# One core, two model blocks and a routed expert layer: sums of squares, scores, weighed values and the router's choice reordered

## The chip, the core and the metric

The kernel runs on one core of a Trainium2 chip. The metric is the device time of one execution in microseconds. Engines: PE is TensorE (PEld its weight loads), DVE is VectorE, ACT is ScalarE, POOL is GpSimd, SP is SyncE, which issues the DMAs. All of them run their own instruction streams and meet only at semaphores.

## What is computed

256 tokens of width 1024, float32, pass through two blocks. The first has a state-space branch (a complex linear scan over 64 groups of 64 states), a dilated attention of three groups of eight heads, and two gates. The second has another recurrent branch, a difference attention and a layer of 32 experts in 4 groups of 8, of which each token uses two of one group.

```
h = rms_norm(x, norm_w);  u, z_s, q, k, v, z_a, r_s, r_a = split(h @ w_in)
y = scan(u) @ C + d_skip * u;  g = gelu(y);  y_s = (g * sigmoid(g @ w_glu) * silu(z_s)) @ w_ssm_out
q, k = rope(rms_norm(q)), rope(rms_norm(k));  y_a = (attention(q, k, v) * silu(z_a)) @ w_attn_out
x = x + (sigmoid(r_s) * y_s + sigmoid(r_a) * y_a) @ w_o
... second block of the same kind, then
g_sel = argmax(xn @ w_rg + b_rg)                    # of 4 groups
e_in_group = (xn @ w_re + b_re)[g_sel]              # 8 logits
top_v, top_i = top_k(e_in_group, 2)
x = x + sum over the two of weight * (silu(xn @ w1[e]) * (xn @ w3[e])) @ w2[e]
```

## The kernel before, in words

All engines' programs are written by hand, each in one order; helper objects give the waits. `Banks` (L112) numbers the uses ("fills") of two PSUM banks: `to_fill` makes PE wait until the fill before on the same bank was read, `filled` and `emptied` signal, `to_read` and `after_read` wait. `pj` has banks 0 and 1, `tp` 2 and 3, `tq` bank 2.

**Start** (L542 to L635, L763 to L788, L949 to L1005). SP issues the first constants, the turned x (1 MB, one semaphore), the first half of u's weights (1 MB, `u_half`), the second half, the state-space matrices and u's second unit. ScalarE issues four small loads (gains of q and k, positions), squares x in four pieces of 512 columns (L619), takes the root of the row sums (L622). DVE multiplies x by the norm gains (L962, `raw`), takes the reciprocal (L966, `rows1`), scales `raw` to `hT` in eight steps (L969) and u's block 0 (L971); then it works through the phases, the rotary angles and the decay factors (L981 to L1005) up to `prm_ready`. PE warms up on constants (L765), sums the squares over the partitions with a matrix of ones (L768, eight products), then makes u in eight blocks (L784): block 0 from `raw`, the rest from `hT`. A float32 product shows as two instructions. ScalarE takes blocks 1 to 7 of u out of PSUM (L629).

**Scan stage** (43 to 240 us). The state-space part goes by 16 pairs. `inputs_of_two_pairs` (L794) and `outputs_of_two_pairs` (L805) run on PE. For each pair ScalarE makes sines and cosines (`trig`, L636 to L642), DVE rotates and scans (L1045 to L1061), POOL turns the states back (L594 to L599) and signals `state_ready`. `trig(n)` waits for `state_ready` of pair n - 2, as its tables are shared by two pairs. Before its first pair, POOL scales the output matrices with the decay factors (L582 to L586): it starts at `prm_ready` and ends with `c_scaled`. Between these, PE makes 26 half units of q, k, v and the gates r (`DENSE`, L323 and L332) in 18 steps h (`HALVES`). ScalarE copies each out (L691), takes the squares of q and k (L695) and their roots (L700); DVE norms and rotates them (`norm_rope`, L1076 to L1084); PE turns them (L856, from h = 5 on, one of 12 in each step), and ScalarE copies them to `qT`, `kT` (L706). The last step, h = 17, makes the last two half units and, between them, the last outputs and `scores(0)`.

**Attention** (248 to 301 us). Eight steps: `scores(a + 1)` (L818), a quarter of z_s (L339), `weigh_values(a - 1)` (L881), `turn_p(a)` (L869). DVE masks, finds the maximum and norms (L1120 to L1131), ScalarE takes exponentials (L667) and copies the turned probabilities (L721), DVE copies the outputs (`take_output`, L1138). Then `weigh_values(7)`, and the eight products of glu (L339).

**Router and experts** (647 us to the end). DVE adds the bias to the logits (L1599) and chooses: `first_largest` (L1602 to L1607) marks the first of the largest values by four linked steps, once for the group and twice for the experts. L1622 writes `aexp`, the 0/1 table of the chosen experts; PE counts places by triangular and full matrices of ones (L1445 to L1449), DVE makes the selection (L1631), PE gathers the tokens (L1512) and multiplies (L1532, L1559, L1564, L1578). The expert weights, 192 MB in units of 2 MB, come through a ring of eight slots; SP's loads L371 and L373 wait until PE has used the units before (`unit_used`). Loads up to the eleventh unit are issued before the router ends.

## Time and profile before

| | |
|---|---|
| median of 3 runs | 1091.53 us (1090.1 to 1091.58) |
| the profiled execution, own time | 1091.93 us |
| its span, first to last instruction | 1090.1 us |
| PE busy | 951.0 us (87%) |
| DVE, ACT, POOL busy | 407.5, 257.3, 157.3 us |
| mean granted clock of PE | 0.939 |
| DMA moved | 292.93 MB, mean 269 GB/s |

The page cuts the span in 40 slices of 27 us; a digit is the busy share in tenths. PE is at 9 until the 25th slice (about 680 us), the DMA row is at 9 from the 23rd to the last but one:

```profile
PE   8999999999999999999999998966665867676756
DMA  9444244242234447643224789999999999999997
```

### The profile page before, as it was taken

Reading aid. Unit: us, or ns where it says so; the run is one execution under the profiler, and the core shown is the slowest. Engines: PE = TensorE matmul, PEld = TensorE weight load, DVE = VectorE, ACT = ScalarE, POOL = GpSimd, SP = SyncE. Lnnn points to the kernel's source line nnn. Section 1 sums busy time; section 2 is a strip of 40 time slices with the busy share of each in tenths; the row PEclk is TensorE's granted clock in tenths of the full one; section 3 lists DMA queues with packets and bytes.
Section 4 is the critical chain, followed back from the end, with each engine's and each line's share of the span. In section 5 each row is a group of like instructions: output and inputs, shape, how many; then the busy total and the mean of one; then the engine's idle time right before and its main releaser. Section 6 shows DMA issues by size and latency. Waiting matters only on the chain.

```text
span 1090.1 us, 12714 instructions
## 1 busy us (share of the span) xinstructions
PE 951.0 (87%) x5108; PEld 560.0 (51%) x5108; DVE 407.5 (37%) x701; ACT 257.3 (24%) x629; POOL 157.3 (14%) x107
## 2 busy tenths in 40 slices
PE   8999999999999999999999998966665867676756
PEld 7655645568888857545788753423221313131312
DVE  6779899836621113263633222210110102020201
ACT  3595977423411021312312020000000000000000
POOL 0976777830000000000000000000000000000000
PEclk9999999999999999999999999988887878897988
DMA  9444244242234447643224789999999999999997
GB/s 356 194 154 154 79 155 155 99 176 85 91 141 155 155 155 256 232 153 125 88 98 155 322 339 378 430 427 423 427 427 425 430 427 429 429 426 429 427 429 313
DMA packets 29777, 292.93 MB, mean 269 GB/s; under 512 B 8480, under 2 KB 9376, under 8 KB 10912
## 3 DMA queue, kind: packets, MB, share of 16 engines
q1 hardware_dynamic: 28640, 292.21, 66.1%
q8 instruction: 33, 0.54, 0.2%
q10 hardware_dynamic: 1088, 0.05, 0.1%
q14 instruction: 16, 0.13, 0.0%
HBM read 291.20 MB, written 1.05 MB: 268 GB/s over the span
## 4 chain that ended last, share of the span: by engine, by line
PE 60%; DMA 32%; ACT 3%; DVE 2%; issue 2%; POOL 1%; SPq 0%; DVEq 0%; ACTq 0%; POOLq 0%
DMA mem<-in_experts 32%; PE psum L332 15%; PE psum L339 8%; PE psum L323 8%; PE psum L311 6%; PE psum L316 5%; PE psum L1532 3%; PE psum L784 3%; PE psum L1858 1%; PE psum L1559 1%; PE psum L818 1%; PE psum L881 1%; PE psum L1549 1%; PE psum L869 1%; PE psum L1512 1%
## 5 line engine op out<-in xcount | busy, mean ns | idle before, releaser
L1532 PE MATMUL psum<-mem 128*32 128x512 f32 x1012 | 151.9, 731 | 79.7 <-DMA mem<-in_experts 79.6
L323 PE MATMUL psum<-mem,hT 128*128 128x512 f32 x288 | 126.3, 595 | 0.8 <-ACT mem L629 0.8
L1532 PEld LDWEIGHTS psum<-mem 128*32 128x32 f32 x1012 | 31.6, 122 | 181.6 <-DMA mem<-in_experts 112.0
L332 PE MATMUL psum<-hT,mem 128*128 128x256 f32 x512 | 115.2, 381 | 0.0
L332 PEld LDWEIGHTS psum<-hT,mem 128*128 128x128 f32 x512 | 95.6, 190 | 15.9 <-issue 2.9
L323 PEld LDWEIGHTS psum<-mem,hT 128*128 128x128 f32 x288 | 55.7, 196 | 64.8 <-issue 64.8
L332 PE MATMUL psum<-mem 128*128 128x256 f32 x320 | 69.7, 379 | 0.0
L311 PE MATMUL psum<-mem,hT 128*128 128x512 f32 x160 | 69.2, 592 | 0.0
L1677 DVE SCALAR_TENSOR_TENSOR mem<-mem,psum 128x512 f32<-128x512 f32 x8 | 5.5, 686 | 158.6 <-ACT mem L1429 158.6
L332 PEld LDWEIGHTS psum<-mem 128*128 128x128 f32 x320 | 60.6, 190 | 8.1
L1559 PE MATMUL psum<-mem 128*32 128x512 f32 x256 | 41.2, 777 | 22.9 <-DMA mem<-in_experts 18.7
L339 PE MATMUL psum<-hT,mem 128*128 128x256 f32 x256 | 57.6, 382 | 0.0
L316 PE MATMUL psum<-mem 128*128 128x512 f32 x128 | 55.6, 592 | 0.0
L1427 ACT ACTIVATE mem<-psum 128x256 f32<-128x256 f32 x8 | 3.1, 384 | 214.6 <-PE psum L1540 214.6
L339 PEld LDWEIGHTS psum<-hT,mem 128*128 128x128 f32 x256 | 48.0, 190 | 7.0
L311 PEld LDWEIGHTS psum<-mem,hT 128*128 128x128 f32 x160 | 30.2, 190 | 36.9 <-issue 36.8
L1061 DVE TENSOR_TENSOR_SCAN mem<-mem 128x512 f32<-128x512 f32 x32 | 49.0, 1569 | 0.0
L1686 DVE TENSOR_TENSOR xres<-xres,psum 128x256 f32<-128x256 f32 (+1 forms) x48 | 24.5, 510 | 54.6 <-PE psum L1549 54.3
L1549 PE MATMUL psum<-mem 128*128 128x256 f32 (+1 forms) x96 | 36.6, 505 | 7.2 <-DVE mem L1682 7.2
L316 PEld LDWEIGHTS psum<-mem 128*128 128x128 f32 x128 | 24.2, 190 | 28.8 <-issue 28.7
L1512 PE MATMUL psum<-mem,xn 128*128 128x128 f32 x256 | 32.7, 289 | 6.6 <-issue 6.4
L1512 PEld LDWEIGHTS psum<-mem,xn 128*128 128x128 f32 x256 | 32.1, 205 | 8.3 <-issue 7.9
(362 smaller groups left out, 1197.3 us busy)
## 6 DMA issues: line engine op xcount, KB each, us to landing
mem<-in_experts SPq DMA_DIRECT2D x86, 2048.0 KB, 35.5
mem<-in_front SPq DMA_DIRECT2D x39, 2048.0 KB, 7.8
mem<-in_experts SPq DMA_DIRECT2D x18, 1024.0 KB, 33.0
mem<-in_front SPq DMA_DIRECT2D x2, 1024.0 KB, 10.3
xn<-in_xT SPq DMA_DIRECT2D x1, 1024.0 KB, 7.1
mem<-in_ssm_b SPq DMA_DIRECT2D x2, 512.0 KB, 12.5
mem<-in_ssm_c SPq DMA_DIRECT2D x2, 512.0 KB, 17.9
xres<-in_x SPq DMA_DIRECT2D x1, 1024.0 KB, 10.0
```

What stands on the lines that cost most here:

```text
L311: ins = pe.matmul(dst, lhs[:, k, P * i:P * i + P], w[:, k, c0:c0 + 512], start=(k == 0), stop=(k == nk - 1))
L316: ins = pe.matmul(dst, lhs[:, k, P * i:P * i + P], w[:, k, c0:c0 + 512], start=(k == 0), stop=(k == lhs.shape[1] - 1))
L323: ins = pe.matmul(dst, tokens[:, k, i], w[:, k, :], start=(k == 0), stop=(k == KD - 1))
L332: ins = pe.matmul(dst[:, at:at + T], w[:, k, P * m:P * m + P], rhs[:, k, :], start=(k == 0), stop=(k == nk - 1))
L339: ins = pe.matmul(dst, w[:, k, P * m:P * m + P], rhs[:, k, :], start=(k == 0), stop=(k == nk - 1))
L784: ins = pe.matmul(pj.tile(s)[:, 0:256], w[:, m, k, :], (hT if s else raw)[:, k, :], start=(k == 0), stop=(k == KD - 1))
L1061: ins = dve.tensor_tensor_scan(out=dst[:, b], data0=decay_[:, 512 * b:512 * b + 512], data1=src, initial=0.0, op0=ALU.mult, op1=ALU.add)
L1512: ins = pe.matmul(bank[:, P * (k % 4):P * (k % 4) + P], xn[:, i, P * k:P * k + P], sel_[:, P * i:P * i + P], start=(i == 0), stop=(i == 1))
L1532: ins = pe.matmul(banks[m // 2 % 2][32 * q:32 * q + 32, :], xgT[:, k, 32 * q:32 * q + 32], w[q][:, FF * kk:FF * kk + FF], start=(k == 0), ...
L1549: pe.matmul(total(n), selT_[:, P * i:P * i + P], y_[:, at:at + width], start=True, stop=True).then_inc(combined, 1)
L1559: ins = pe.matmul(banks[2][r, :], hidT[:, k, r], w[q][:, 512 * kk:512 * kk + 512], start=(k == 0), stop=(k == 3), tile_position=(0, 32 * q))
L1686: dve.tensor_tensor(dst, dst, total(n), ALU.add).then_inc(added, 1)
```

## The change

1. The sum of squares: x arrives by two halves (`xT_in[0]`, `xT_in[1]`), u's first blocks by two loads of 512 KB (`u_block_in`). DVE adds the four pieces of squares to one (three additions of 512 columns, `sq_added`), and PE needs two products with ones for it, behind u's block 0. Block 1 too is made from `raw` and scaled by DVE (`scale_u`). Warm-up products: five, not six. The gains of q and k come with the constants, so three of ScalarE's four small loads are gone; the first constants are 56 KB shorter.
2. PE's waits on the last two blocks of u and on `c_scaled` ahead of step h = 0 move to h = 2 and to the first outputs; ScalarE's on `c_scaled` to its first copy into `qT`.
3. In step 17 the last outputs stand ahead of the last half unit, and `scores(0)` between its two blocks.
4. `weigh_values(7)` stands behind the first product of glu.
5. The router ranks: for each logit the number of larger ones, and equal ones of lower index, is summed; rank 0 is the first choice, rank below 2 the two chosen. The table of places takes two products with 64 columns where three had 32. What the weights need (maxima, differences) comes behind the selection, and the weights' chain behind the first gathered tokens.

```diff
         def sync_of_first_layer(sp):
...
-            sp.dma_start(x_turned, A["xT"]).then_inc(xT_in, 16)
-            sp.dma_start(ring[:, 0, 0:2048], A["front"][0, :, 0:2048]).then_inc(u_half, 16)
+            for n in range(2):
+                sp.dma_start(x_turned[:, 4 * n:4 * n + 4, :], A["xT"][:, 4 * n:4 * n + 4, :]).then_inc(xT_in[n], 16)
+            for n in range(2):
+                sp.dma_start(ring[:, 0, 1024 * n:1024 * n + 1024], A["front"][0, :, 1024 * n:1024 * n + 1024]).then_inc(u_block_in[n], 16)
...
         def scalar_of_first_layer(act):
-            for c, name in enumerate(("q_norm_w", "k_norm_w")):
-                act.dma_start(qkw[:, 3 * c:3 * c + 3, :], A[name][0, :, 0:16].partition_broadcast(P)).then_inc(misc_in, 16)
-            act.dma_start(qk_col, A["qk_columns"]).then_inc(misc_in, 16)
             act.dma_start(posi[:, :], A["att_positions"]).then_inc(misc_in, 16)
...
-            for j in range(1, 4):
+            for j in range(2, 4):
                 take_u(j)
...
-            act.wait_ge(c_scaled, 1)
-            act.wait_ge(misc_in, 64)
+            act.wait_ge(con2_in, 16)
...
                         tq.to_read(act, s)
+                        if s == 0:
+                            act.wait_ge(c_scaled, 1)
...
-            for n in range(6):
+            for n in range(5):
                 pe.matmul(banks[7][:, 0:256], ident, con[:, 0:256], start=True, stop=True)
-            for k in range(KD):
-                pe.wait_ge(sq_done, k // 2 + 1)
-                ins = pe.matmul(tp.tile(TP_X)[:, 0:256], C("ones"), squares[:, 256 * k:256 * k + 256], start=(k == 0), stop=(k == KD - 1))
-            tp.filled(ins, TP_X)
+            def sum_of_squares():
+                pe.wait_ge(sq_added, 3)
+                for k in range(2):
+                    ins = pe.matmul(tp.tile(TP_X)[:, 0:256], C("ones"), squares[:, 256 * k:256 * k + 256], start=(k == 0), stop=(k == 1))
+                tp.filled(ins, TP_X)
...
-            for m in range(4):
+            project_u(0, 0)
+            sum_of_squares()
+            for m in range(1, 4):
                 project_u(0, m)
...
-            for s in range(2):
-                pj.after_read(pe, PJ_U + 6 + s)
-            pe.wait_ge(c_scaled, 1)
             for h in range(STEPS):
+                if h == 2:
+                    for s in range(2):
+                        pj.after_read(pe, PJ_U + 6 + s)
...
                 for d in dense_of(h):
-                    if h == STEPS - 1 and d == dense_of(h)[1]:
-                        outputs_of_two_pairs(PAIRS // 2 - 1)
-                        for s in range(2):
-                            tq.after_read(pe, 10 + s)
-                        scores(0)
                     w = unit_ready(pe, DENSE[d // 2])
                     s = PJ_QKV + d
                     pj.to_fill(pe, s)
-                    if DENSE[d // 2][0] in "qkv":
+                    if h == STEPS - 1 and d == dense_of(h)[1]:
+                        outputs_of_two_pairs(PAIRS // 2 - 1)
+                        project_turned(pe, w, (2 * (d % 2),), pj.tile(s), hT)
+                        for q in range(2):
+                            tq.after_read(pe, 10 + q)
+                        scores(0)
+                        ins = project_turned(pe, w, (2 * (d % 2) + 1,), pj.tile(s), hT)
+                    elif DENSE[d // 2][0] in "qkv":
...
+            pe.wait_ge(g_ready, 2)
+            glu_gate(0)
             weigh_values(ATT_STEPS - 1)
-
-            pe.wait_ge(g_ready, 2)
-            for m in range(8):
...
+            for m in range(1, 8):
+                glu_gate(m)
...
+                for n in range(2):
+                    dve.wait_ge(sq_done, 2 * n + 2)
+                    a, b = (squares[:, 512 * m:512 * m + 512] for m in (2 * n, 2 * n + 1))
+                    dve.tensor_tensor(a, a, b, ALU.add).then_inc(sq_added, 1)
+                dve.wait_ge(sq_added, 2)
+                dve.tensor_tensor(squares[:, 0:512], squares[:, 0:512], squares[:, 1024:1536], ALU.add).then_inc(sq_added, 1)
...
+                scale_u(0)
                 for k in range(KD):
                     dve.tensor_tensor(hT[:, k, :], raw[:, k, :], rows1, ALU.mult).then_inc(hT_ready, 1)
-                pj.to_read(dve, PJ_U)
-                pj.emptied(dve.tensor_tensor(uT[:, 0, :], pj.tile(PJ_U)[:, 0:256], rows1, ALU.mult), PJ_U)
+                scale_u(1)
...
+            def ranks(out, x, n, lower, beats):
+
+                larger, equal = beats[:, :, :, 0], beats[:, :, :, 1]
+                other, own = bc(x.unsqueeze(2), [P, 2, n, n]), bc(x.unsqueeze(3), [P, 2, n, n])
+                mark(dve.tensor_tensor(equal, other, own, ALU.is_equal), dve3)
+                link(dve, dve.tensor_tensor(larger, other, own, ALU.is_gt), dve3)
+                first = bc(lower.rearrange("p (e f) -> p e f", e=n).unsqueeze(1), [P, 2, n, n])
+                step(dve.tensor_tensor(equal, equal, first, ALU.mult))
+                step(dve.tensor_reduce(out, beats.rearrange("p i e v f -> p i e (v f)"), AX.X, ALU.add))
...
-            step(dve.tensor_reduce(m1, eg, AX.X, ALU.max))
-            first_largest(oh1, eg, m1, C("rev8"), 8, t8)
-            step(dve.scalar_tensor_tensor(out=eg2, in0=oh1, scalar=NEG, in1=eg, op0=ALU.mult, op1=ALU.add))
-            step(dve.tensor_reduce(m2nd, eg2, AX.X, ALU.max))
-            first_largest(oh2, eg2, m2nd, C("rev8"), 8, t8)
-            step(dve.tensor_tensor(s8, oh1, oh2, ALU.add))
-            dve.tensor_tensor(by_group(aexp), bc(s8.unsqueeze(2), [P, 2, 4, 8]), of_group, ALU.mult).then_inc(chosen, 1)
...
+            ranks(rank, eg, 8, C("lower8"), beaten)
+            for i in range(2):
+                dve.scalar_tensor_tensor(out=by_group(aexp)[:, i], in0=bc(rank[:, i].unsqueeze(1), [P, 4, 8]), scalar=2.0,
+                                         in1=of_group[:, i], op0=ALU.is_lt, op1=ALU.mult).then_inc(chosen, 1)
```

## Rows read from the trace of the kernel before

**Rows 1.** Stretches: us, busy us (instructions) of PE, PEld, DVE, ACT, POOL, granted clock, DMA share, GB/s.

```profile
100.00:200.00 100.00, 99.56 (x450) 59.31 (x452) 91.76 (x105) 75.14 (x205) 77.40 (x53) 1.00 0.36 129
800.00:1000.00 200.00, 134.38 (x888) 43.99 (x888) 22.48 (x40) 7.59 (x17) 0.00 (x0) 0.80 1.01 428
```

**Rows 2.** PE's waits: line, released by, us in total, times, longest.

```profile
PE psum L1445 <- DVE mem L1622: 1.2, 1, 1.2
PE psum L323 <- ACT mem L629: 0.8, 1, 0.8
PE psum L881 <- ACT mem L721: 0.8, 1, 0.8
PE psum L818 <- ACT mem L691: 0.8, 1, 0.8
PE psum L856 <- ACT mem L706: 0.4, 1, 0.4
```

**Rows 3.** Time order, the start: start, duration, engine, line, operation, count [idle before].

```profile
4.42 5.49 PE L765 MATMUL psum<-con 128*128 128x256 f32 x12 [4.42 <-DMA con<-in_constants]
9.70 4.08 PE L768 MATMUL psum<-mem,con 128*128 128x256 f32 x16
...
13.61 3.62 PE L784 MATMUL psum<-xres,mem 128*128 128x256 f32 x16
...
14.32 1.75 DVE L966 RECIPROCAL mem<-mem 128x256 f32<-128x256 f32 x1 [3.76 <-ACT mem L622]
...
18.80 0.42 DVE L971 TENSOR_TENSOR mem<-psum,mem 128x256 f32<-128x256 f32 x1
```

**Rows 4.** Issue to landing of L544 (x, from 1.2) and L545 (u, from 1.7).

```profile
DMA to landing us min/median/max: 7.1/7.1/7.1
DMA to landing us min/median/max: 9.2/9.2/9.2
```

**Rows 5.** Time order, the chain beside PE, 28 to 113 us.

```profile
28.17 2.23 POOL L582 TENSOR_TENSOR mem<-mem 128x1024 f32<-128x1024 f32 x1 [27.72 <-DVE mem L1005]
...
51.60 1.60 POOL L599 TENSOR_TENSOR mem<-mem 128x512 f32<-128x512 f32 x1
...
53.31 0.62 ACT L636 ACTIVATE mem<-small 128x510 f32<-128x510 f32 x1
...
91.83 1.72 POOL L594 TENSOR_TENSOR mem<-mem 128x512 f32<-128x512 f32 x1 [7.56 <-issue]
...
102.85 0.63 ACT L636 ACTIVATE mem<-small 128x510 f32<-128x510 f32 x1 [4.69 <-POOL mem L599]
...
112.37 0.63 PE L856 MATMUL psum<-con,xres 128*128 128x128 f32 x4 [0.44 <-ACT mem L706]
```

**Rows 6.** Time order of PE in the expert stage.

```profile
758.84 3.24 PE L1532 MATMUL psum<-mem 128*32 128x512 f32 x16 [2.98 <-DMA mem<-in_experts]
```

**Rows 7.** Stretches of half a microsecond around it, columns as in rows 1.

```profile
758.00:758.50 0.50, 0.00 (x0) 0.00 (x0) 0.00 (x0) 0.00 (x0) 0.00 (x0) 0.64 1.08 459
761.00:761.50 0.50, 0.50 (x8) 0.00 (x0) 0.00 (x0) 0.00 (x0) 0.00 (x0) 0.50 0.92 393
```

**Rows 8.** Time order around the first scores.

```profile
238.72 1.15 PE L818 MATMUL psum<-mem 64*128 64x256 f32 x12
...
242.71 0.72 ACT L667 ACTIVATE mem<-mem,small 128x512 f32<-128x512 f32 x1 [8.68 <-DVE small L1124]
...
247.01 0.60 ACT L691 ACTIVATE mem<-psum 128x512 f32<-128x512 f32 x1 [2.30 <-PE psum L332]
```

**Rows 9.** DVE's copy of the last weighed values.

```profile
301.56 0.30 DVE L1138 COPY mem<-psum 128x128 f32<-128x128 f32 x1 [2.66 <-PE psum L881]
```

**Rows 10.** Time order of DVE in the router.

```profile
652.88 0.27 DVE L1615 TENSOR_REDUCE mem<-mem 128x16 f32<-128x64 f32 x1
...
655.67 0.23 DVE L1622 TENSOR_TENSOR mem<-mem 128x64 f32<-128x64 f32 x1
```

**Rows 11.** The microsecond of the expert stage's first ring load, columns as in rows 1.

```profile
663.00:664.00 1.00, 1.00 (x16) 0.28 (x11) 0.00 (x0) 0.00 (x0) 0.00 (x0) 1.00 0.00 0
```

More of the change, by code:

```diff
@@ L81, in constants @@
     put("ones", 1.0)
-    put("rev4", 4.0 - np.arange(4)[None, :])
-    put("rev8", 8.0 - np.arange(8)[None, :])
+    for n in (4, 8):
+        put(f"lower{n}", np.tri(n, n, -1).reshape(1, n * n))
     return c
@@ L440, in build @@
         ropcos = small[:, 582:598].rearrange("p (i n) -> p i n", i=2)
-        hss = [small[:, 972 + 16 * n:988 + 16 * n] for n in range(3)]
+        hss = [small[:, 148 + 16 * n:164 + 16 * n] for n in range(3)]
         hrs = [small[:, 646 + 16 * n:662 + 16 * n] for n in range(3)]
@@ L781, in project_u @@
                         pe.wait_ge(raw_ready, k + 1)
[L782 removed]
+                    elif s == 2:
                         pe.wait_ge(hT_ready, k + 1)
[L784 removed]
+                    ins = pe.matmul(pj.tile(s)[:, 0:256], w[:, m, k, :], (raw if s < 2 else hT)[:, k, :], start=(k == 0), stop=(k == KD - 1))
                 pj.filled(ins, s)
@@ L801, in outputs_of_two_pairs @@
                     pe.wait_ge(y_free.sem, j)
+                else:
+                    pe.wait_ge(c_scaled, 1)
                 for n, (CT, H) in enumerate(((CTr, Hr), (CTi, Hi))):
@@ L1649, in vector_of_experts @@
             step(dve.tensor_tensor(p1, p1, gw, ALU.mult))
-            for n in range(2):
-                dve.wait_ge(gather_full, n + 1)
-                take(2 * n, 2, banks[2 + 2 * n], xg_low)
             step(dve.tensor_tensor(p2, p1, ediff, ALU.mult))
```

96 lines of the change are left out of this document (55 added, 41 removed).

## The prediction

> **What bounds the kernel now.** I read the table of stretches first. From about 665 us on the DMA engines are busy all the time (share 1.01) while TensorE (PE) is busy two thirds of it; between 100 and 200 us it is PE that is full, 99.56 of 100 us [rows 1]. So the span is a PE stage of some 650 us followed by a stage that only streams expert weights. A microsecond saved in front of the stream moves the end by a microsecond if it lets PE issue or release something earlier, or the stream start earlier. The list of PE's waits shows what is to be had in front: 0.8 us at the first q projection (L323), 0.4 us at the turning of q and k (L856), 0.8 us at the scores (L818) and 0.8 us at the weighed values (L881) [rows 2]. After that I read the time order around each edited place, and, because a wait of PE that is removed is worth only what the next one leaves, the chain of work between 28 and 112 us.
>
> **Start: sum of squares on DVE, u's first block ahead of it.** Before, 12 warm-up matmuls (6 products, two passes each) run from 4.42 to 9.70, 0.44 us apart, 16 sum-of-squares instructions run until 13.61, and then 64 instructions of u follow, 16 in 3.46 us [rows 3]. After, there are 10 warm-ups (until 8.8), 16 of u's block 0, 4 of the sum. Block 0 needs the first 512 KB of u; its first 1024 KB landed 9.2 us after an issue at 1.7, at 10.9, and the 1024 KB of x ahead of them 7.1 after 1.2, at 8.3 [rows 4]: 2.6 us for 1024 KB. 512 KB less is 1.3 us; the shorter constants and the missing small loads of ScalarE's queue may give 0.2 to 0.7 more. So I take 9.0 for its start (8.8 to 9.9). The 16 instructions from 9.70 to 13.61 fit 0.43 us each until 10.6 and 0.216 after: there PE's clock rose from 1.2 to 2.4 GHz, after it had worked without a stop from 4.42. The 20 instructions then end at 10.6 + (20 - 3.7) x 0.216 = 14.1 instead of 13.6, and block 2 starts at 17.6 instead of 13.61 + 2 x 3.46 = 20.5. **PE is 2.9 us ahead** (2.3 to 3.1). The three additions of 512 columns (0.69 us each, two of them 0.6 apart) end at 11.7 on a DVE that was idle then: they cost nothing, and would cost from 13 us on. The removal of the waits on the last reads of u and on `c_scaled` at 43.5 adds what PE waited there, the 0.8 us of [rows 2]; the first product that comes after needs only u's last block but one to be read, which ScalarE did 2 us earlier. PE would be some 3.5 us ahead (3.1 if a part of that wait stays).
>
> **But the chain beside PE gets later.** The row factor comes 0.5 us later (14.1 against 13.6), its reciprocal is 1.75 us as before, and two blocks of u (0.42 us, 0.35 apart) are now scaled by DVE where one was [rows 3]. What follows on DVE without a pause ends in `prm_ready`, so that is 0.5 + 0.35 = **0.85 us later** (0.6 to 1.6). GpSimd (POOL) sat idle for 27.7 us until exactly that, at 28.17, and then works without a pause to the end of its first pair at 51.60 + 1.60 = 53.20; ScalarE's `trig(2)` starts at 53.31, because it needs that pair [rows 5]. From there ScalarE, then DVE (through 91.7), then POOL's fifth pair from 91.83, ScalarE's `trig(6)` from 102.85 (4.69 us idle for POOL) and its copy L706 follow each other, and at 112.37 PE waits 0.44 us for that copy [rows 5]. None of them waits for PE on the way after 53.3. An earlier PE doesn't make them earlier: it arrives between 108.4 and 108.8 and waits. A later POOL makes them later; some of the 0.85 is given back, as POOL's third pair starts on a DVE that is not late, so I take **+0.6 us** at 112 (0 to +1.5). The whole lead is thus lost there, and PE's stop is 0.4 + 3.3 + 0.6 = 4.3 us long (a little of it may fall earlier, at a bank that ScalarE copies late).
>
> **What the stop costs beyond itself.** In the last stage PE stood still for 2.98 us, until 758.84 [rows 6], and the granted clock went from 1.00 to 0.50 (1.2 GHz) within the half microsecond from 758.0 and was still there between 761.0 and 761.5 [rows 7]. At 1.2 GHz a matmul takes double (0.43 against 0.216 us, above). The stop of 1.2 us at L1445 [rows 2] left the clock at 1.00. A stop of 4.3 us lies above both, so I expect the clock to fall in it and about 3 us of work to be done at half pace: **+1.5 us** (0 to 3). The Trainium skill (TensorE: Matmul & The Clock Gate, What's actually happening) says that the throttled state is the default and that activity releases it, which speaks against a change that moves PE's waits into one long one; by it the cost would be as above, without it 0. The rows agree with it.
>
> **First scores inside the last projection.** Before: last outputs, scores(0) at 238.72, then 32 instructions of projection. After, 16 of those (3.46 us) go ahead of the scores. Neither PE nor anybody else waited at 238.72. But ScalarE stands behind it: it does nothing for 8.68 us until the maximum of these scores is there, takes the exponentials at 242.71, and only then copies the last two projections; the second copy started at 247.01, when PE delivered [rows 8]. Now the exponentials start at 246.17, the two copies at 247.60 and 248.10, and end at 248.70 instead of 247.61. PE waits for the second (`after_read` ahead of scores(1)), so its 0.8 us of [rows 2] become 1.9: **+1.1 us** (0.9 to 1.2). DVE's part has 5 us of slack ahead of the first turned probabilities, so nothing else follows.
>
> **Last weighed values behind a gate product.** PE waited 0.85 us for ScalarE's copy at 300.43; now 16 instructions of glu (3.46 us) cover that, and the bank they write is that of the weighed values before, emptied by then. But the second glu product needs the bank of these weighed values, which DVE empties by a 0.30 us copy right after them [rows 9]. Before, glu 0 stood between; now nothing does: 0.04 + 0.30 + 0.13 = 0.47 us of wait. **-0.4 us** (-0.85 to 0).
>
> **Router by ranks.** From the end of the reduction L1615 at 653.15 to the end of L1622 at 655.90 DVE makes 13 steps in 2.75 us [rows 10]. After: compare, compare, multiply on 128 elements each (between the 0.23 us of 64 and the 0.42 of 256: 0.30), a reduction of 256 to 16 elements (64 took 0.27; no row has 256 so: 0.45 to 0.6), two writes of 32 elements (0.19). With 0.035 us between linked steps and an overlap of 0.08 between unlinked ones: 0.22 + 0.33 + 0.33 + 0.5 + 0.3 = 1.7. The group rank costs as much as the first largest (1.0 against 1.06). PE's table of places needs 4 instructions instead of 6 (-0.2). `sel_ready` comes 1.0 - 0.06 + 0.2 = **1.15 us earlier** (0.5 to 1.5). This counts although the stream bounds: the load that waits for the second expert unit was issued at 663.13, and in 663 to 664 us the DMA engines moved nothing [rows 11]; the hole was 1.8 us. It shrinks by the gain, and all later issues go with PE.
>
> **Sum.** +0.6 + 1.5 + 1.1 - 0.4 - 1.15 = +1.65 us. The profiled execution took 1091.93 us, 1.8 around a span of 1090.1, and would take 1093.6; it lies 0.4 above the median of 1091.53, so I predict a median of **1093.2 us**.
>
> **Rivals.** *The clock holds through the stop*: all else as above, +0.15, 1091.7. For it: no row shows a stop of just this length. *PE keeps its lead*: if the chain at 112 is not binding, -3.5 + 1.1 - 0.4 - 1.15 = -3.95, 1087.6. For it: PE's stage is 99.5% full [rows 1] and the wait at 112 was only 0.4 us, so a slightly quicker POOL frees part. Against it: `trig(2)` can't start before POOL's first pair, whatever PE does. *The clock rises late at the start* (slower than before): between the warm-ups and u's block 0 PE stands still for 0.2 to 1 us before its clock has risen. If the rise comes 3.4 us later for that (as long as the low stretch of [rows 7], 758.1 to 761.5), the 20 instructions end 1.7 us later, at 15.8, DVE and POOL with them, and 112 us is reached at +2.3: in all +3.35, 1094.9. It decides as soon as block 0 lands after the last warm-up. *The stream hides the router*: if its start goes by landing times and not by the issue at 663.13, the 1.15 us fall away: +2.8, 1094.3. Against it: the hole of [rows 11].
>
> **Chances.** Forecast 0.38, clock holds 0.18, lead kept 0.17, late rise 0.14, router hidden 0.13. About 0.2% (2.2 us) is what a measurement of this kernel can tell from no change. Faster by more: the lead kept and a little of the second, 0.19. Slower by more, above 1093.7: a third of the forecast's own spread (1091.9 to 1094.7), most of the last two: 0.34. Within: 0.47. The range takes the upper half of the lead-kept case and the late rise with one microsecond of spread: 1088.5 to 1096.0.
>
> **What would show it.** At the start: block 0 of u from about 9 us, the sum's 4 instructions ending near 14, block 2 at 17.6. POOL's first instruction at 29.0. No wait of PE at 40, but one of 4 us for L706's successor near 109 to 113, with a granted clock of 0.5 behind it. ScalarE's last two copies adjoining near 248.6 and a PE wait of 1.9 us ahead of scores(1). 0.5 us ahead of the second glu product. The select of the first group 1.1 us nearer to the logits, and a DMA hole of 0.7 us. The prediction is wrong above all if `trig(2)` starts before 53 us of the old time scale, or if PE's long wait is absent.

## The result: slower by half a per cent, and the profile after

The changed kernel takes 1097.77 us (median of five runs; the kernel before 1091.29 beside it), ratio 1.0055, 95% interval 1.0043 to 1.0067. One of the five runs took 1186.88 us at a lower mean clock and is not in the ratio. The prediction said 1093.2, with a range of 1088.5 to 1096.0. The profiled span grew from 1090.1 to 1095.9 us.

**The start.** Time order of the kernel after (start us, duration us, engine, line, operation, count, idle before and what ended it); it answers to [rows 3] and to the first of [rows 5]:

```profile
3.29 4.64 PE L774 MATMUL psum<-con 128*128 128x256 f32 x10 [3.29 <-DMA con<-in_constants]
9.72 6.67 PE L795 MATMUL psum<-xres,mem 128*128 128x256 f32 x16 [1.80 <-DMA mem<-in_front]
16.23 1.03 PE L779 MATMUL psum<-mem,con 128*128 128x256 f32 x4
17.09 3.62 PE L795 MATMUL psum<-xres,mem 128*128 128x256 f32 x16
20.55 7.09 PE L795 MATMUL psum<-hT,mem 128*128 128x256 f32 x32
...
17.80 1.75 DVE L993 RECIPROCAL mem<-mem 128x256 f32<-128x256 f32 x1 [6.60 <-ACT mem L630]
...
31.98 2.22 POOL L593 TENSOR_TENSOR mem<-mem 128x1024 f32<-128x1024 f32 x1 [31.53 <-DVE mem L1037]
```

The warm-ups start 1.1 us earlier than before and end at 7.93; u's block 0 has landed only at 9.72. Behind the hole of 1.80 us the block takes 6.67 us, where the next one, with as many instructions, takes 3.62: nearly all of it ran at half pace. So the sum of squares ends at 17.2, the reciprocal starts at 17.80 instead of 14.32, and POOL at 31.98 instead of 28.17: **3.8 us late**. 3.5 of them are there at the reciprocal; the scaling of a second block adds 0.3 (13.85 us from reciprocal to POOL before, 14.18 after). Block 2 starts at 20.55; worked out for the kernel before it was 20.5. PE's lead is nil.

**The turn near 112 us.** First four rows of the kernel before that none of the groups above has, in the same form:

```profile
119.71 7.07 PE L332 MATMUL psum<-hT,mem 128*128 128x256 f32 x32
247.75 1.15 PE L818 MATMUL psum<-mem 64*128 64x256 f32 x12 [0.78 <-ACT mem L691]
656.91 0.42 DVE L1631 TENSOR_TENSOR mem<-con,psum 128x256 f32<-128x256 f32 x1 [0.87 <-PE psum L1447]
659.43 0.62 PE L1532 MATMUL psum<-hT,mem 128*32 128x512 f32 x2
```

and the kernel after, time order at the same places:

```profile
57.44 0.63 ACT L644 ACTIVATE mem<-small 128x510 f32<-128x510 f32 x1 [5.11 <-POOL mem L610]
...
72.68 7.14 PE L338 MATMUL psum<-hT,mem 128*128 128x256 f32 x32 [1.21 <-ACT xres L698]
...
116.10 1.09 PE L873 MATMUL psum<-con,xres 128*128 128x128 f32 x4 [3.78 <-ACT mem L715]
116.98 9.30 PE L329 MATMUL psum<-mem,hT 128*128 128x512 f32 x16
126.12 4.05 PE L338 MATMUL psum<-hT,mem 128*128 128x256 f32 x18
...
255.40 1.15 PE L831 MATMUL psum<-mem 64*128 64x256 f32 x12 [1.82 <-ACT mem L698]
...
312.19 3.05 PE L345 MATMUL psum<-mem 128*128 128x256 f32 x13 [0.49 <-DVE mem L1170]
...
666.46 0.62 PE L1568 MATMUL psum<-hT,mem 128*32 128x512 f32 x2 [1.00 <-DMA hT<-in_experts]
```

`trig(2)` starts at 57.44 (53.31 in [rows 5]), the turn at 116.10 (112.37): the 3.8 us of POOL arrive there whole, as +3.73. PE stands still for 3.78 us ahead of it. Its wait of 0.85 us at 43.52, which the second edit was to remove, is gone, but a wait of 1.21 us at 72.68 has come for it: PE reaches the turn at 112.32, and had reached it at 111.93 before. The granted clock of the stretches behind (us from and to, length, busy and count of PE, clock, DMA share, GB/s):

```profile
113.00:115.00 2.00, 0.00 (x0) 0.93 0.00 0
115.00:117.00 2.00, 0.90 (x5) 0.50 0.00 0
```

It fell to 0.50 (1.2 GHz) in the stop, and the next projection starts at 126.12 instead of 119.71, +6.41: the clock costs another 2.7 us in this execution. At the second scores it is 255.40 against 247.75, +7.65, so the moved scores cost 1.2 more. The wait of the second glu product is 0.49 where PE had waited 0.85 for the weighed values.

**The router.** DVE's selection starts 4.29 us after the second logits (658.59 to 662.88) instead of 5.57 (651.34 to 656.91): 1.28 us gained. But the first product on expert weights waits 1.00 us for the landing of its weights and comes at 666.46 against 659.43, +7.03. Nearly all the gain is gone within 4 us: the logits were 7.25 us late, so 0.2 is left of it. At the end of the span +5.8 is left; the other 1.2 us lie in the streaming stage. In the ninth run below a kernel that starts its first expert unit at the same 659.42 as the kernel before ends 0.9 us earlier, so single executions differ by that much there; what makes the 1.2 us is open.

### The profile page after: what moved, and what is told of

It reads as the page before. It is cut to its first block, busy times and chain, and to the rows that moved or that the text cites. A ratio compares the mean times of both kernels' runs of the same rounds, so it can differ in the third digit from the quotient of the medians.

```text
span 1095.9 us, 12684 instructions
## 1 busy us (share of the span) xinstructions
PE 948.0 (87%) x5092; PEld 558.9 (51%) x5092; DVE 406.9 (37%) x705; ACT 257.1 (23%) x628; POOL 157.6 (14%) x107
## 4 chain that ended last, share of the span: by engine, by line
PE 56%; DMA 33%; POOL 3%; DVE 3%; ACT 2%; issue 2%; SPq 0%; DVEq 0%; POOLq 0%; ACTq 0%
DMA mem<-in_experts 32%; PE psum L338 15%; PE psum L345 8%; PE psum L329 7%; PE psum L317 6%; PE psum L322 5%; PE psum L1568 3%; PE psum L1901 1%; PE psum L1595 1%; PE psum L831 1%; PE psum L898 1%; PE psum L1585 1%; PE psum L886 1%; DMA hT<-in_experts 1%; DMA mem<-in_front 1%
## 5 line engine op out<-in xcount | busy, mean ns | idle before, releaser
L1568 PE MATMUL psum<-mem 128*32 128x512 f32 x1012 | 146.3, 707 | 84.4 <-DMA mem<-in_experts 84.4
L329 PE MATMUL psum<-mem,hT 128*128 128x512 f32 x288 | 128.5, 603 | 0.0
L317 PE MATMUL psum<-mem,hT 128*128 128x512 f32 x160 | 69.2, 592 | 0.0
L1595 PE MATMUL psum<-mem 128*32 128x512 f32 x256 | 43.7, 819 | 20.7 <-DMA mem<-in_experts 17.2
```

Source lines behind the costliest of these rows:

```text
L317: ins = pe.matmul(dst, lhs[:, k, P * i:P * i + P], w[:, k, c0:c0 + 512], start=(k == 0), stop=(k == nk - 1))
L329: ins = pe.matmul(dst, tokens[:, k, i], w[:, k, :], start=(k == 0), stop=(k == KD - 1))
L1568: ins = pe.matmul(banks[m // 2 % 2][32 * q:32 * q + 32, :], xgT[:, k, 32 * q:32 * q + 32], w[q][:, FF * kk:FF * kk + FF], start=(k == 0), ...
L1595: ins = pe.matmul(banks[2][r, :], hidT[:, k, r], w[q][:, 512 * kk:512 * kk + 512], start=(k == 0), stop=(k == 3), tile_position=(0, 32 * q))
```

## The experiments

Each was timed in at least five runs beside the kernel before; all ratios are to the kernel before unless said otherwise. Rows and waits are those of one profiled execution of each kernel, so they tell how that execution went; the ratios tell what the kernels cost. Where two are compared, each carries an interval of about 0.001.

### First run: the start of the kernel before

```diff
-            for n in range(5):
+            for n in range(6):
                 pe.matmul(banks[7][:, 0:256], ident, con[:, 0:256], start=True, stop=True)
+            for k in range(KD):
+                pe.wait_ge(sq_done, k // 2 + 1)
+                ins = pe.matmul(tp.tile(TP_X)[:, 0:256], C("ones"), squares[:, 256 * k:256 * k + 256], ...)
+            tp.filled(ins, TP_X)
...
-            project_u(0, 0)
-            sum_of_squares()
-            for m in range(1, 4):
+            for m in range(4):
                 project_u(0, m)
```

(with the one load of x, the first 1024 KB of u in one load, and block 1 from `hT`.)

> The changed kernel with the start of the kernel before (x and u's first 1024 KB by one load each, six warm-up products, eight products of squares ahead of u's block 0, ScalarE takes block 1); the moved waits, the scores, the weighed values and the router stay changed. Theory (the loss comes from the start: the sum of squares ends 3.5 us late, so POOL, ScalarE and PE's turn near 112 us are late, and the stop lets the clock fall): POOL's first instruction near 28.2, PE's stop at the turn 1.0 to 1.3 us at 112.4 with the clock at 1.00 behind it, and against the kernel before +1.2 (scores) -0.4 (weighed values) -0.2 to -1.15 (router): 1091.0 to 1091.9 us, ratio 0.9997 to 1.0006. Rival A (the moved scores and the removed waits make the loss): about 1097, ratio 1.005. Rival B (the router pays in full and the scores cost nothing): 1089.8, ratio 0.9986.

Measured: ratio 0.9981 (0.9972 to 0.9990), 1089.67 us. Time order:

```profile
11.61 3.62 PE L790 MATMUL psum<-xres,mem 128*128 128x256 f32 x16
...
26.18 2.23 POOL L589 TENSOR_TENSOR mem<-mem 128x1024 f32<-128x1024 f32 x1 [25.73 <-DVE mem L1022]
...
109.94 0.63 PE L866 MATMUL psum<-con,xres 128*128 128x128 f32 x4 [1.11 <-ACT mem L711]
110.40 7.04 PE L329 MATMUL psum<-mem,hT 128*128 128x512 f32 x16
```

The whole loss of the change, 0.0074 as ratio or 8 us, is in its start. The stop at the turn is 1.11 us as expected and the 16 instructions behind it take 7.04. The run is 1.3 us faster than I had expected at best. The constants (56 KB shorter, three small loads of ScalarE gone) land 1.1 us earlier than in [rows 3] here too, and nothing behind them waits for u: block 0 starts at 11.61 against 13.61. The other 0.9 us are the clock, which rose sooner here (12 warm-up instructions in 5.01 us instead of 5.49); in the eighth and ninth run, which have the start of the kernel before, block 0 starts at 13.12 and 12.37, so this part differs between executions. The earlier constants are a gain which I had not seen as one; which of the two edits brings it, no run tells. Rival A falls: with moved scores and removed waits in place there is no loss. Rival B's 0.9986 lies within the interval, but its reasons don't hold in the trace: PE waits 1.82 us ahead of the second scores, as the theory has it, and the selection comes 5.50 us after the logits, as before the change.

### Second run: two more warm-up products

```diff
-            for n in range(5):
+            for n in range(7):
                 pe.matmul(banks[7][:, 0:256], ident, con[:, 0:256], start=True, stop=True)
```

> The changed kernel with seven warm-up products instead of five, so that PE works without a hole from 3.3 us until u's block 0 has landed at 9.7. Theory (the clock rises late because of the 1.8 us hole, and that makes everything behind the sum of squares late): the clock rises near 9.5 instead of 16.2, the 4 instructions of the sum end at 14.2 instead of 17.1, DVE's reciprocal starts near 14.9 instead of 17.8, POOL near 29.1 instead of 32.0, the turn near 113.2 instead of 116.1. PE is 2.9 us earlier too, so its stop stays 3.8 us and the clock still falls: 2.9 us less than the changed kernel, ratio 0.9973 to it. Rival (POOL's and PE's chains have slack at the start, the loss arises later): no difference. Rival (the rise goes by time since the start and not by the hole): block 0 at half pace as before, 16.2 for the rise, no difference.

Measured: ratio 1.0033 (1.0021 to 1.0045), 1094.89 us. Time order:

```profile
3.33 5.18 PE L774 MATMUL psum<-con 128*128 128x256 f32 x14 [3.33 <-DMA con<-in_constants]
9.97 3.72 PE L795 MATMUL psum<-xres,mem 128*128 128x256 f32 x16 [1.45 <-DMA mem<-in_front]
...
29.28 2.22 POOL L593 TENSOR_TENSOR mem<-mem 128x1024 f32<-128x1024 f32 x1 [28.83 <-DVE mem L1037]
...
113.38 1.08 PE L873 MATMUL psum<-con,xres 128*128 128x128 f32 x4 [3.76 <-ACT mem L715]
114.26 8.11 PE L329 MATMUL psum<-mem,hT 128*128 128x512 f32 x16
```

POOL and the turn come 2.7 us earlier than in the kernel after, and 2.4 us of the time are back (1.0055 less 1.0033); both rivals fall. The stop stays at 3.76 us and the clock falls (0.50 between 113 and 115 us). From the turn to the next projection it is 8.83 us (113.38 to 122.21) where the kernel before takes 7.34, so the fall costs 1.5 us here.

One detail went otherwise: the hole is still there, 1.45 us long, because the clock rose within the warm-ups (14 instructions in 5.18 us, where 10 had taken 4.64). Two things are thus different from the kernel after, that the hole began behind the rise and that it is shorter, and this run alone can't part them. The next three runs, with five warm-up products, can. There too the clock rose within the warm-ups, 10 instructions in 3.90, 3.87 and 4.31 us (4.64 at half pace throughout), and yet block 0 behind the hole ran wholly or mostly at half pace: 5.41 us behind a hole of 2.06, 6.64 behind 3.39, 5.41 behind 2.49 (third, fourth and fifth run), and the granted clock is 0.50 from 11 to 13 us in all three. So a rise ahead of the hole isn't enough; the clock falls again if the hole is long. Of the six profiles of this start the two with holes of 1.45 and 1.08 us (this run and the eleventh, seven warm-ups) kept the pace, the four with holes of 1.80 to 3.39 us did not.

This run comes nearest to what my forecast had described, and it costs 3.6 us, not 1.65; the turn is 1.0 us late where I had 0.6. Its trace has another loss that the forecast lacks, behind the moved scores; the third run shows the same one, and its rows stand there.

The Trainium skill (TensorE: Matmul & The Clock Gate, What's actually happening) says that the throttled state is the default and that the point of the transition varies from run to run. The rows agree that it varies: equal warm-ups of 12 instructions took 5.49 us in the kernel before, 5.01 in the first run and 4.28 in the tenth.

### Third run: constant products in the stop

```diff
                         pe.wait_ge(qk_ready.sem, w + 1)
+                        if s == 1:
+                            pe.wait_ge(y_free.sem, 2)
+                            for n in range(8):
+                                pe.matmul(banks[3][:, 256:512], ident, con[:, 0:256], start=True, stop=True)
                         tq.to_fill(pe, s)
```

> The changed kernel with eight products on constants (16 instructions, 3.5 us at full clock, into an unused half of a PSUM bank) where PE stands still for 3.8 us ahead of the turn at 116.1 us. Nothing else differs. Theory (the fall of the clock in the stop costs about 2.4 us beyond the stop): the turn still starts at 116.1, the granted clock stays at 1.00, the 16 instructions behind it take 7.0 instead of 9.3 us, the end is 2.4 us earlier, ratio 0.9978 to the changed kernel. Rival (the clock's part is given back later, at a copy of ScalarE or a load): no difference, though the clock holds.

Measured: ratio 1.0029 (1.0018 to 1.0039), 1093.92 us. Time order:

```profile
3.96 3.90 PE L774 MATMUL psum<-con 128*128 128x256 f32 x10 [3.96 <-DMA con<-in_constants]
9.92 5.41 PE L795 MATMUL psum<-xres,mem 128*128 128x256 f32 x16 [2.06 <-DMA mem<-in_front]
...
111.08 3.62 PE L873 MATMUL psum<-con 128*128 128x256 f32 x16
114.97 0.66 PE L877 MATMUL psum<-con,xres 128*128 128x128 f32 x4 [0.27 <-ACT mem L715]
115.46 7.04 PE L329 MATMUL psum<-mem,hT 128*128 128x512 f32 x16
...
251.61 1.15 PE L831 MATMUL psum<-mem 64*128 64x256 f32 x12 [1.82 <-ACT mem L698]
252.69 5.41 PE L345 MATMUL psum<-hT,mem 128*128 128x256 f32 x16
```

and of its table of stretches, at the start:

```profile
11.00:13.00 2.00, 2.00 (x6) 0.50 0.99 408
```

The clock holds at the turn, and the stretch behind it takes 7.04 instead of 9.30 us. The ratio is 0.0026 lower, 2.8 us, where 2.4 were expected. The turn itself came at 114.97 in this execution, 1.1 us earlier, since the half pace in block 0 ended sooner (5.41 against 6.67 us); how much of the 2.8 us is that, the ratio can't tell. From turn to next projection it is 7.36 us (114.97 to 122.33) against 10.02 in the kernel after: **2.66 us for the fall** in that execution, against 1.5 in the second run and 1.6 in the fifth.

The last two rows of the time order show a loss that I had not priced. The 1.82 us that PE waits ahead of the second scores, where the change had moved the first ones, can drop the clock too: the 16 instructions of z_s behind them take 5.41 us here, at a granted clock of 0.50 between 254 and 256 us, and as long in the second and fifth run, 3.72 in the kernel after, and PE is 1.7 us later for it. The same wait of 1.82 us stands in seven profiles, and the clock fell in three of them (second, third and fifth run) and held in four (the kernel after, first, fourth and ninth run). What decides it, no run shows.

### Fourth run: decay factors ahead of the rotary angles

```diff
             angle_sums(0)
-            rope_angles()
             decay_factors()
+            rope_angles()
```

> The changed kernel with DVE's decay factors ahead of its rotary angles (10 instructions, 2.0 us), nothing else. PE, x, u and the sum of squares are as in the changed kernel; only POOL's release comes 2.0 us earlier. Theory (the chain POOL, trig, copy, turn sets PE's stop): POOL's first instruction at 30.0, ScalarE's trig(2) near 55.5, the turn at 114.1 with a stop of 1.8 us; the end 2.0 us earlier if the clock still falls there, 4.4 us earlier if it holds: ratio 0.9960 to 0.9982 to the changed kernel. Rival (the stop at the turn is set by PE's own lead or by another chain, not by POOL's start): no difference, the turn stays at 116.1.

Measured: ratio 1.0066 (1.0052 to 1.0079), 1099.28 us. Neither of the two. Time order of DVE and of POOL from 30.7 us, then of PE:

```profile
30.93 3.85 DVE L1043 TENSOR_SCALAR small<-con,small 128x8 f32<-128x8 f32 x2
35.02 2.21 DVE L1045 TENSOR_SCALAR small<-small 128x16 f32<-128x16 f32 x1
37.26 3.85 DVE L1050 SCALAR_TENSOR_TENSOR small<-small 128x16 f32<-128x16 f32 x3
...
34.83 2.37 POOL L595 TENSOR_TENSOR mem<-mem 128x1024 f32<-128x1024 f32 x1
37.27 1.94 POOL L593 TENSOR_TENSOR mem<-mem 128x1024 f32<-128x1024 f32 x1
...
49.17 11.26 PE L329 MATMUL psum<-mem,hT 128*128 128x512 f32 x20 [5.60 <-ACT mem L637]
```

The rotary angles had taken 2.0 us in all. Beside POOL they take 10.6 us, from 30.73 to 41.33: two instructions on 8 elements alone 3.85 us. They end where an instruction of POOL ends and the next begins (34.78 and 34.83, 37.23 and 37.27). So POOL's release came earlier and DVE's first scan much later, and PE stood still for 5.60 us at 43.6. The question of the run stays unanswered by it; the fifth was made to ask it again. The Trainium skill (SBUF — State Buffer, SBUF: two separate sides) says that GpSimd and some instructions of DVE (those with two inputs in SBUF, or in a mode that takes two ports) share a pair of ports as an exclusive lock for a whole instruction, the other side waiting. These rows agree with the waiting; and in the kernel after DVE's instructions of 512 columns with an input in PSUM took their usual 0.68 us at 33.14 and 34.33 us, beside POOL's.

### Fifth run: rotary angles ahead of the row scaling

```diff
             gains_onto_input()
+            rope_angles()
             scale_rows()
...
             angle_sums(0)
-            rope_angles()
             decay_factors()
```

> The changed kernel with DVE's rotary angles (10 instructions, 2.0 us) moved from behind the scaling of the rows to ahead of it, where DVE stands idle for 6.6 us waiting for ScalarE's root. Unlike the run with the decay factors first, no small instruction of DVE lands beside POOL's. Theory (POOL's release sets the stop at the turn): POOL's first instruction at 30.0, the turn at 114.1 after a stop of 1.8 us, and because stops of 1.2 us left the clock alone the 16 instructions behind it take 7.0 us: 2.0 to 4.4 us less than the changed kernel, ratio 0.9960 to 0.9982 to it, 0.9995 to 1.0040 to the kernel before. Rival (another chain sets the stop): the turn stays at 116.1 and the ratio to the kernel before stays near 1.005.

Measured: ratio 1.0029 (1.0019 to 1.0040), 1094.65 us, 0.9974 of the kernel after by the two ratios. Time order:

```profile
29.50 2.22 POOL L593 TENSOR_TENSOR mem<-mem 128x1024 f32<-128x1024 f32 x1 [29.04 <-DVE mem L1052]
...
113.27 1.09 PE L873 MATMUL psum<-con,xres 128*128 128x128 f32 x4 [3.02 <-ACT mem L715]
114.15 8.27 PE L329 MATMUL psum<-mem,hT 128*128 128x512 f32 x16
```

POOL's release moved by 2.5 us (0.6 of them from a sooner rise of the clock), the turn by 2.8, with PE's own work as it was: the chain from POOL to the turn is real. But the stop is 3.02 us, not 1.8. PE had waited 1.2 us for ScalarE at 72.7 us in the kernel after and does so no more, so it too came earlier; and a stop of 3.02 us still lets the clock fall (8.27 us instead of 7.04). The ratio to the kernel after, 0.9974, lies in the stretch that I had expected (0.9960 to 0.9982), but neither the stop of 1.8 us nor the held clock is why.

### Sixth run: old start and old place of the first scores

The first run's kernel with

```diff
+                    if h == STEPS - 1 and d == dense_of(h)[1]:
+                        outputs_of_two_pairs(PAIRS // 2 - 1)
+                        for s in range(2):
+                            tq.after_read(pe, 10 + s)
+                        scores(0)
                     w = unit_ready(pe, DENSE[d // 2])
```

> The first run's kernel (old start) with the first scores too where the kernel before has them. What stays of the change: the constants and small loads, the moved waits, the weighed values, the router. Theory (moving the scores costs what ScalarE's copies behind the exponentials add): PE's wait ahead of scores(1) is 0.8 instead of 1.8 us, the end 1.2 us earlier than with the moved scores: ratio 0.9970 to the kernel before. Rival (the 1.2 us vanish in a later wait): ratio 0.9981, as in the first run.

Measured: ratio 0.9966 (0.9954 to 0.9978), 1088.07 us, **faster than both kernels**. Time order:

```profile
245.78 1.15 PE L826 MATMUL psum<-mem 64*128 64x256 f32 x12 [0.78 <-ACT mem L694]
```

The wait is 0.78 us again. The ratios of the sixth and the first run differ by 0.0015, 1.6 us, with intervals that overlap; 1.2 were expected.

### Seventh run: the rotary angles moved in the sixth run's kernel

The edit is that of the fifth run.

> The kernel of the sixth run with DVE's rotary angles ahead of the row scaling as well, in the 3.8 us in which DVE waits for the root. Theory: POOL's first instruction at 24.2 instead of 26.2, the chain at the turn would be ready at 107.9, PE comes at 108.8 and doesn't wait: another 1.1 us, ratio 0.9960 to the kernel before. Rival (the next chain waits at once, or POOL's earlier work slows DVE's by the shared use of memory): ratio 0.9970, the stop of 1.1 us is there or has moved.

Measured: ratio 0.9957 (0.9943 to 0.9970), 1087.22 us. Time order:

```profile
24.75 2.22 POOL L589 TENSOR_TENSOR mem<-mem 128x1024 f32<-128x1024 f32 x1 [24.30 <-DVE mem L1035]
...
109.72 0.63 PE L864 MATMUL psum<-con,xres 128*128 128x128 f32 x4 [0.45 <-ACT mem L711]
```

POOL starts 1.9 us earlier than in the sixth run (26.63 there), but the turn only 0.67 (110.39 there), and a wait of 0.45 us is left, so another link takes over. By the ratios the gain is 1 us within intervals that overlap. It is the fastest of the kernels measured, 0.43% below the kernel before.

### Eighth run: the router alone

The kernel before with the router's part of the change.

> The kernel before with the router's ranks and its two products for the table of places, and nothing else. From the second logits to the first selection: 5.57 us before, 4.29 in the changed kernel, but 5.50 and 5.23 in the first two runs, where PE's eight constant products ahead of the table took 5.3 and 5.0 instead of 3.7 us. Theory (the gain of 1.28 us is there only while these products run at full clock): either 1.28 us earlier selection with products of 3.7 us, or under 0.3 us with products above 5 us. Of 1.28 at the selection the end gets 0.2 to 1.28: ratio 0.9988 to 0.9998. Rival (the router's stage gets slower by what is now queued behind the selection): ratio above 1.000.

Measured: ratio 0.9988 (0.9979 to 0.9997), 1090.38 us. Time order:

```profile
650.82 0.26 DVE L1606 SCALAR_TENSOR_TENSOR mem<-psum,small 128x36 f32<-128x36 f32 x1 [1.56 <-PE psum L2028]
655.11 0.42 DVE L1640 TENSOR_TENSOR mem<-con,psum 128x256 f32<-128x256 f32 x1 [0.52 <-PE psum L1453]
658.77 0.62 PE L1538 MATMUL psum<-hT,mem 128*32 128x512 f32 x2 [1.07 <-DMA hT<-in_experts]
```

4.29 us from logits to selection, at full clock. Logits 0.52 us earlier than before, selection 1.80, first expert product 0.66: of the 1.28 us gained 0.14 pass the landing of the first unit. The time says 1.3 us gained, with an interval from 0.3 to 2.3; what of this is the router's, against the 0.5 us by which this execution was early, the two views leave open. The second half of the theory is seen in the first run, where the clock was down in the router's constant products:

```profile
649.54 5.32 PE L1464 MATMUL psum<-con 128*128 128x256 f32 x16
...
655.35 0.42 DVE L1655 TENSOR_TENSOR mem<-con,psum 128x256 f32<-128x256 f32 x1 [1.73 <-PE psum L1468]
```

The granted clock was 0.50 there between 650 and 652 us. The selection came 5.50 us after the logits, as late as before the change (5.57): the ranks had made PE's eight products the bound, which DVE's longer work had covered by 1.2 us ([rows 2], L1445).

### Ninth run: the scores alone

The kernel before with the last outputs and `scores(0)` inside the last half unit.

> The kernel before with the first scores and the last outputs moved into the last projection, and nothing else. Theory: ScalarE's exponentials and behind them its last two copies come later, PE waits 1.8 instead of 0.8 us ahead of scores(1), 1.2 us later at the end (the first and the sixth run differ by 0.0015): ratio 1.0011 to the kernel before. Rival (the difference of those two runs was chance, the later waits of the attention stage take it up): ratio 1.0000, scores(2) and later at the old times.

Measured: ratio 1.0010 (1.0001 to 1.0019), 1091.8 us. Time order:

```profile
247.73 1.15 PE L818 MATMUL psum<-mem 64*128 64x256 f32 x12 [1.82 <-ACT mem L691]
```

The turn came at 111.11 in this execution and at 112.37 before, and yet the second scores are at the old 247.7: 1.24 us lost between, with the wait of 1.82 us. The term is there in the trace; the time agrees with 1.1 us, but with an interval from 0.1 to 2.1.

### Tenth run: five constant products in the router

The seventh run's kernel with

```diff
-            for n in range(8):
+            for n in range(5):
                 pe.matmul(banks[6][:, 0:256], ident, con[:, 0:256], start=True, stop=True)
```

> The seventh run's kernel with five constant products ahead of the router's table instead of eight. In three of the profiles so far the clock was down there, the eight products took 5.0 to 5.3 instead of 3.7 us and DVE waited 1.5 to 1.7 us for PE's table. Theory (these products have become the bound in such executions): at half clock five take 3.3 to 4.3 us and the selection comes up to 1.2 us earlier; at full clock PE stands still for 1.3 us behind them and nothing changes. Mean gain 0 to 0.6 us, ratio 0.9952 to 0.9957 to the kernel before. Rival (fewer products leave the clock down or let it fall): table and gathers at half pace, 1 to 3 us later, ratio 0.997 to 0.999.

Measured: ratio 0.9975 (0.9964 to 0.9985), 1088.36 us. The profiled execution had the clock at 1.00 there, and PE stood still for 1.4 us ahead of the table. Its turn came 1.2 us earlier than the seventh run's (108.55 against 109.72), as its warm-ups ran faster, and its span is only 0.3 us shorter. The time is longer by 0.0018, with intervals that just overlap. No gain, then; whether in other executions the clock stays low, as the rival says, this one profile doesn't show.

### Eleventh run: all three causes mended in the changed kernel

Seven warm-ups, the filled stop and the old place of the first scores.

> The changed kernel with all three causes mended at once: seven warm-up products (second run), the eight products in the stop at the turn (third run), the first scores where the kernel before has them (sixth run). The changed start stays. Theory (the three causes add up to the whole loss): ratio of the changed kernel 1.0055, less 0.0027 (2.9 us of the rise), 0.0022 (2.4 us of the fall), 0.0011 (the scores): 0.9995 to the kernel before, 0.9987 to 1.0003 allowing for the rise; the turn at 113.4 with no stop over 0.5 us and the clock at 1.00 behind it. That is still 3 us above the sixth run (0.9966), because the turn comes 3 us later than its 110.4: the sum of squares behind u's block 0 costs that by itself. Rival (a fourth cause, or causes that overlap): ratio above 1.001.

Measured: ratio 1.0006 (0.9997 to 1.0015), 1091.41 us. Time order:

```profile
10.29 3.72 PE L795 MATMUL psum<-xres,mem 128*128 128x256 f32 x16 [1.08 <-DMA mem<-in_front]
...
113.62 0.66 PE L875 MATMUL psum<-con,xres 128*128 128x128 f32 x4 [0.22 <-ACT mem L715]
```

The 16 instructions behind the turn take 7.04 us again, and 0.0049 of the 0.0055 are gone. With the scores back in their old place the wait ahead of the second ones is 0.78 us, and the clock holds there too. The rest to the sixth run's 0.9966 is 0.0040, 4.4 us; 3.2 of them are the turn at 113.62 against 110.39. The sum of squares behind u's block 0 is the cause by the rows: block 0 starts at 10.29 and the sum's 4 instructions end at 14.9; in the sixth run the sum had ended at 12.2. No run moved the sum alone. The other 1.2 us lie within the intervals of the two ratios, and I have no account of them.

## Why the prediction was wrong, point by point

**The start, the step that failed.** "So I take 9.0 for its start", and "the 20 instructions then end at 10.6 + (20 - 3.7) x 0.216 = 14.1". The first number was 9.72 here and 9.9 to 10.6 in five other profiles of this start; I had worked it out from bytes and the constants' old landing, and let the constants gain nothing for the warm-ups: they ended at 7.93, not 8.8. With that the hole that I had priced only in a rival was certain. The second number took the clock's rise at 10.6 from an unbroken row of work and kept it for a broken one; the 20 instructions ended at 17.2. So +0.6 at the turn became +3.7, and the lead of 2.9 us nothing. The second run shows it: with the rise ahead of block 0 the turn is at 113.38, +1.0. The rival *the clock rises late* had the mechanism right; its chance, 0.14, was too low and so was its price: I had put the sum's end at 15.8 and the turn at +2.3. Its condition, that it decides as soon as block 0 lands behind the last warm-up, was too wide: in the second and eleventh run block 0 does so and the pace holds. The 0.35 us for the second block scaled by DVE were right (0.33).

**The clock in the stop.** Mechanism right, and the size within the 0 to 3 stated, though not the 1.5: 2.66 us in the kernel after, measured against the third run. I had let it rise again after 3 us of work; it stayed at 0.50 until 121, 5 us behind the stop. In the second and fifth run it was back after 3 us and the cost was 1.5 and 1.6, so which of the two sizes comes changes from one execution to the next. The length of the stop, 4.3 us, was near the 3.8 by accident: PE was not 3 us early but the chain 3.7 us late. The second run, with the chain on time and PE early, had 3.76.

**"An earlier PE doesn't make them earlier, a later POOL makes them later."** Right: +3.8 at POOL, +4.1 at `trig(2)`, +3.7 at the turn; and the fifth run, in which only DVE's order and so POOL's release was moved, moved the turn by as much. The rival *PE keeps its lead* falls with it.

**First scores**, +1.1: 1.2 in the trace, 0.0010 as ratio (ninth run). Right, wait by wait: exponentials, two copies, 1.8 us. What I put at nothing without a reason is the clock behind this wait: where it falls (three of the seven profiles with the moved scores, not that of the kernel after) another 1.7 us go.

**Removed waits**, 0.8 for PE: the wait at 43.5 went, one of 1.21 us at 72.7 came. With the chain late it would have been worth nothing at the turn in any case.

**Weighed values**, -0.4: the wait is 0.49 instead of 0.85. Right in the trace; too small to be told by the time, and no run was given to it.

**Router.** The steps were right (1.15 forecast, 1.28 measured), the place where they pay was not. I had let "all later issues go with PE" and looked at the hole at 663 us, but not at the landing of the first unit, whose load waits for the end of the logits and not for the choice. It takes back all but 0.1 to 0.3 us. The rival *the stream hides the router* had the outcome for another reason. That PE's constant products become the bound at half clock I had not seen.

**The sum.** +3.7 +2.7 +1.2 -0.4 -0.2 = +7.0 at the first expert product, +5.8 at the end, against +1.65. Of the 5.4 us of error in this execution the start has 3.1, the fall of the clock 1.2 and the router 0.95.

## What to carry to other kernels

Before you put work that waits for a transfer between warm-up products and the first real ones, compare the landing with the warm-ups' end at its earliest, and price half pace into everything that hangs on the first result, even if the clock should have risen within the warm-ups: two more products on constants were worth 2.4 us here (0.0022, with an interval of about 0.0017), and eight in a later stop kept the clock up, worth 1.5 to 2.7 us. Ask of every wait that an edit lengthens whether the clock will hold through it, also when it is under 2 us. An engine that starts last on a chain (POOL here, idle for 28 us) is the one to feed; ordering a neighbour's small instructions ahead of its work was worth up to 1 and up to 3 us (seventh run, within its interval, and fifth run, with 0.6 us of faster warm-ups in it), and having them beside its work cost PE a stop of 5.6 us (fourth run). A gain in a choice pays only up to the next landing that doesn't depend on the choice.

## What the runs showed of the hardware that I had not expected

- DVE's instructions on 8 to 16 elements took 1.3 to 2.2 us each beside POOL's, by the mean of their groups, and about 0.2 without them (fourth run against the kernel after); three groups of them lasted until just then an instruction of POOL ended.
- Stops of PE at 1.00 that left the clock there: 1.08 to 1.45 us, and 1.82 in four profiles. Stops that dropped it to 0.50: 1.82 in three others, 2.06, 2.49, 3.02, 3.39, 3.76, 3.78 and 5.60. So a stop of one and the same length and place did either. (All of these lie ahead of the expert stage.)
- At the very start the column of the granted clock says 1.00 between 9 and 17 us, while 16 instructions take 6.67 us there and 3.62 later. The pace there has to be read from durations. It isn't always so: in the third, fourth and fifth run the column says 0.50 at 11 to 13 us.
- Equal warm-ups, begun within 0.1 us of each other, ran at half pace for different times: 12 instructions in 5.46, 5.01 and 4.28 us (sixth, first and tenth run). That alone moves what follows by up to 1.2 us from one execution to the next (turn at 109.72 in the seventh run and at 108.55 in the tenth, whose kernels are the same until the router).
- In three of thirteen profiles (first, second and fifth run) the clock was at 0.50 around the router's constant products, in the others at 1.00, seven of which have the same program there.
